# Output projection by column halves, expert weights loaded into the homes that come free, and a router that chooses in one pass

## The chip, the cores and the metric

The kernel runs on one core of a Trainium2 chip. The metric is device microseconds (us) of one execution; the median of several executions is compared. One core has a matrix engine (TensorE, in the rows PE, its weight loads PEld), a vector engine (VectorE, DVE), an activation engine (ScalarE, ACT), GpSimd (POOL) and a queue engine (SyncE, SP) that issues most transfers. All of them run their own instruction streams and wait for each other through semaphores.

## The reference

Two transformer blocks run one after the other on 512 tokens of width 1024, in float32. What matters here is the end of the second block: the output projection of its mixer, and a mixture of 32 experts in 4 groups of 8.

```python
h = h + z @ w_o                                   # mixer's output projection, 1024 x 1024
u = rmsnorm(h, norm_ffn_g)
g_logits = u @ w_group + b_group                  # 4 groups
p_grp, g_sel = top_k(softmax(g_logits), 1)
e_logits = (u @ w_router + b_router).reshape(n, 4, 8)
in_grp = e_logits of the chosen group             # 8 experts
p_exp, e_sel = top_k(softmax(in_grp), 2)
gate = p_grp * p_exp / sum(p_exp)
out[token] += gate * ((silu(x @ w1[e]) * (x @ w3[e])) @ w2[e])   # for both chosen experts
return rmsnorm(h, norm_final_g)
```

Each expert's w1, w3 and w2 are 2 MB each (1024 x 512 or 512 x 1024 in float32).

## The kernel before

Nearly all of SBUF is one array `M` of 128 partitions by 53200 words; every tile is a fixed stretch of it, a "home" (`at(offset, shape)`), so whether a transfer can start is a question of who last used its home. 1 MB is 2048 words of every partition. PSUM is `PS`, 8 banks of 512 words.

**Output projection (`out_pe`, `out_act`, `out_dve`).** The 512 tokens are NT = 4 tiles of 128. For each tile and each half of the 1024 output columns there is one job (`HN_JOBS`, the tile outermost): `rows` makes 8 products with `WO` (each appears as two matrix rows in the trace, L2964) and adds the residual `hT` by 4 small products with the identity (L2967). ACT copies the bank into `HN` (L3010), and after the second half of a tile makes the root mean square of the row (square, Ln, table load, Exp: L3016 to L3020); DVE scales the row into `UN` (L3044), and ACT stores it to `u_rows` in HBM (`store`, L3006). Between the jobs PE turns a finished tile (`turn`, 8 transposes, L2976), DVE copies the turned tile to `UT` (L3035), and PE makes its 36 router and group logits (`logits`, L2983). The last two tiles' turns and logits stand behind the last job. Then all four engines meet at a barrier (`stage`, L257).

**Routing (`route_dve`, `route_pe`).** DVE finds for all tiles the best group, then the best and second-best expert in it (`first_best`, L3216 to L3220, three times; one instruction each, followed by a wait for its result), and gives the chosen experts as ones in `ES` (L3237, `routing_given`). PE counts them by matrix products (L3185, L3187), DVE works out each token's slot, PE names the rows of each pair of experts (L3193), DVE writes the list (L3291, L3292), and POOL gathers the first pair's rows from `u_rows` (L3404). While PE waits it runs `keep_busy`: products with the identity whose result nobody reads (L356; 6 calls are 12 matrix rows).

**Experts (`experts_sp`, `experts_pe`).** Expert k and expert k + 16 form a pair; each takes 64 rows, so a pair fills the array's 128 columns. There are 16 pairs here. `w1_w3` makes the w1 product and signals `h_one`, then the w3 product and signals `h_done`; `w2` turns the hidden rows, multiplies by w2 and signals `y_done`. All three are L3443 in the trace. w1 has two homes (`W1B[0]`, `W1B[1]`), w3 and w2 have one each. So SP issues the next pair but one's w1 at `h_one`, the next pair's w3 at `h_done`, and its w2 at `y_done`: 12 MB a pair. Pair 0's w1 and w3 are issued at the start of the output projection. Pair 1's w3 goes to three 1 MB homes named `SPARE` and, for its last megabyte, to W3B after pair 0's `h_done`:

```python
sp.wait_ge(stage_done, WORKERS * (PROJ2_STAGE + 4))   # behind the output projection
gate_weights(1, (1, BASE + 1), of=(0,))               # 2 MB
sp.wait_ge(u_stored, U_STORED)
down_weights((0, BASE))                               # 4 MB
sp.wait_ge(g_in, 16)                                  # the first rows are gathered
...                                                   # GFIN 0.5 MB, w1 2 MB, two spares 2 MB
sp.wait_ge(stage_done, WORKERS * (PROJ2_STAGE + 5))
spare_part(2, 1, 1)                                   # 1 MB
```

**End.** SP loads the experts' rows back (`CG`, 4 x 1 MB, L3617), DVE adds them weighted (L3578), normalises with `GFIN` (L3572), and SP stores the output.

Of the kernel before, what the change touches and what calls it, by code (L numbers as in the profile page):

```python
# [23 lines left out]
P = 128  # L24
# [100 lines left out]
def gain_columns(inputs):  # L125
# [9 lines left out]
    bias = np.concatenate([np.asarray(inputs["b_group_2"])[0], np.asarray(inputs["b_router_2"])[0]])  # L135
# [60 lines left out]
def program(nc, I, out, dbg=None, stop=99):  # L196

    ctx = ExitStack()
    with ctx:
# [1600 lines left out]
        WO = at(WORK0 + 5280, KD, D)  # L1800
# [1155 lines left out]
        HN_JOBS = [(t, half) for t in range(NT) for half in range(2)]  # L2956
# [3 lines left out]
        def out_pe(pe):  # L2960
            def rows(n, t, half):
                lo = OUT_TILES[t][0]
                for a in range(KD):
                    nc.tensor.matmul(PS[:, n % 2, :], ZT[:, a, lo:lo + P], WO[:, a, 512 * half:512 * half + 512],  # L2964
                                     start=a == 0, stop=False)
                for a in range(4):
                    last = nc.tensor.matmul(PS[:, n % 2, a * P:a * P + P], hT[:, 4 * half + a, lo:lo + P], ident,  # L2967
                                            start=False, stop=a == 3)
                last.then_inc(hn_ready, 1)

            def turn(t):
                pe.wait_ge(hn_free, 2 + 2 * t + 2)
                if t >= 2:
                    pe.wait_ge(ut_out, t - 1)
# [3 lines left out]
                last.then_inc(ut_ready, 1)  # L2978

            def logits(t):  # L2980
                pe.wait_ge(ut_out, t + 1)
                for a in range(KD):
                    last = nc.tensor.matmul(PS[:, 6, 36 * t:36 * t + 36], UT[:, a, P * t:P * t + P], RW[:, a, :],  # L2983
                                            start=a == 0, stop=a == KD - 1)
                last.then_inc(lg_ready, 1)

            pe.wait_ge(wo_in, 16)
            for n, (t, half) in enumerate(HN_JOBS):
                pe.wait_ge(hn_free, n + 1)
                rows(n, t, half)  # L2990
                if half == 0 and t >= 2:
                    logits(t - 2)
                if half == 1 and t >= 1:
                    turn(t - 1)
            turn(NT - 1)
            logits(NT - 2)
            logits(NT - 1)

        def out_act(act):
# [8 lines left out]
            for n, (t, half) in enumerate(HN_JOBS):  # L3008
                act.wait_ge(hn_ready, n + 1)
                nc.scalar.activation(HN[:, t, 512 * half:512 * half + 512], PS[:, n % 2, :], ACT.Copy).then_inc(hn_free, 1)  # L3010
                if half == 0:
                    if t > 0:
                        store(t - 1)
                    continue
                act.drain()
# [9 lines left out]
        def out_dve(dve):  # L3025
# [6 lines left out]
            def turned(t):  # L3032
                dve.wait_ge(ut_ready, t + 1)
                for c in range(2):
                    nc.vector.tensor_copy(UT[:, 4 * c:4 * c + 4, P * t:P * t + P],  # L3035
                                          PS[:, 2 + 2 * (t % 2) + c, :].rearrange("p (a n) -> p a n", n=P))
                dve.drain().then_inc(ut_out, 1)

            for t in range(NT):
                if t == NT - 1:  # L3040
                    turned(NT - 2)
                    turned(NT - 1)
# [3 lines left out]
                if 0 < t < NT - 1:  # L3046
                    turned(t - 1)


        def mix2_sp(sp):  # L3050
# [3 lines left out]
            sp.dma_start(WO, I["w_o_2"].rearrange("(a p) n -> p a n", p=P)).then_inc(wo_in, 16)  # L3054
# [23 lines left out]
        def mix2_dve(dve):  # L3078
# [7 lines left out]
            out_dve(dve); stage(dve, "dve")  # L3086
# [5 lines left out]
        XG, YO = at(HT0, D), at(HT0 + 1024, D)  # L3092
        UT = at(XN0, KD, S1)
        W1B = [[at(WORK0 + 18592 + 4096 * k, KD, DE) for k in range(2)], [at(XN0, KD, DE), at(WORK0 + 8192, KD, DE)]]
        W3B = [at(WORK0 + 26784 + 4096 * k, KD, DE) for k in range(2)]
        W2B = [at(WORK0 + 4096 * k, 4, D) for k in range(2)]
        SPARE = [at(WORK0 + 12288, 4, DE), at(HT0 + 2048, 4, DE), at(RG0 + 2560, 4, DE)]
        UN = [at(RG0, D), at(RG0 + 1024, D), at(WORK0, D), at(WORK0 + 13472, D)]
        JUNK = at(HT0, D)
# [12 lines left out]
        LG = small(NT, 36)  # L3112
        OHG, GE = small(NT, 4), small(NT, 4)
        EL, EL2, OH1, OH2 = small(NT, 8), small(NT, 8), small(NT, 8), small(NT, 8)
# [4 lines left out]
        C5 = {n: small(NT) for n in ("gmax", "gsum", "mx", "m1", "m2", "ex", "den", "ga1", "ga2", "ss", "rs")}  # L3119
        C10 = {n: small(2 * NT) for n in ("rank", "pair", "half", "ob", "q", "in", "eid", "step", "last")}  # L3120
# [5 lines left out]
        CG = [at(base + 2 * D * n, 2, D) for base in (XN0, WORK0 + 8192) for n in range(2)]  # L3126
        GFIN = GROW
        LAST_SLOTS = [at(HT0 + 2048 + P * n, P) for n in range(2 * NT)]
        LAST_GATES = at(HT0 + 3072, S1)
# [31 lines left out]
        def route_sp(sp):  # L3161
            sp.wait_ge(stage_done, WORKERS * (PROJ2_STAGE + 3))
            sp.dma_start(GROW, I["norm_ffn_g_2"].to_broadcast([P, D])).then_inc(rw_in, 16)
            sp.dma_start(RW[:, :, 0:4], wcols("w_group_2", 0, 4)).then_inc(rw_in, 16)
            sp.dma_start(RW[:, :, 4:36], wcols("w_router_2", 0, 32)).then_inc(rw_in, 16)
# [14 lines left out]
        def route_pe(pe):  # L3180
            keep_busy(6, 7)
# [17 lines left out]

        def route_dve(dve):  # L3200
# [6 lines left out]
            dve.wait_ge(lg_ready, NT)  # L3207
            for t in range(NT):
                stt(LG[:, t, :], PS[:, 6, 36 * t:36 * t + 36], C5["rs"][:, t:t + 1], g["router_bias"], ALU.mult, ALU.add)
            nc.vector.memset(ES[:, NT, :], 0.0)  # L3210
            dve.drain()
            G, EG = LG[:, :, 0:4], LG[:, :, 4:36].rearrange("p t (g e) -> p t g e", g=4)

            def first_best(values, best, order, n, dest, place):

                then(nc.vector.reduce_max(best, values, axis=AX))  # L3216
                then(tt(dest, values, bc(best, n), ALU.is_equal))
                then(tt(dest, dest, over(order, NT), ALU.mult))
                then(nc.vector.reduce_max(place, dest, axis=AX))
                then(tt(dest, dest, bc(place, n), ALU.is_equal))  # L3220


            first_best(G, C5["gmax"], C["g4"], 4, OHG, C5["mx"])

            T4 = T48.rearrange("p t (g e) -> p t g e", g=4)
            then(tt(T4, EG, OHG.unsqueeze(3).to_broadcast([P, NT, 4, 8]), ALU.mult))
            then(nc.vector.reduce_sum(EL, T48.rearrange("p t (g e) -> p t e g", g=4), axis=AX))
            first_best(EL, C5["m1"], C["g8"], 8, OH1, C10["eid"][:, 0:NT])
            then(stt(EL2, OH1, -BIG, EL, ALU.mult, ALU.add))
            first_best(EL2, C5["m2"], C["g8"], 8, OH2, C10["eid"][:, NT:2 * NT])  # L3230

            for j, oh in enumerate((OH1, OH2)):
                tt(E12[:, j].rearrange("p t (g e) -> p t g e", g=4), OHG.unsqueeze(3).to_broadcast([P, NT, 4, 8]),
                   oh.unsqueeze(2).to_broadcast([P, NT, 4, 8]), ALU.mult)
            ts_(STEP64, C["iota"][:, 1:9], float(ROWS), None, ALU.mult)
            dve.drain()
            tt(ES[:, 0:NT, :], E12[:, 0], E12[:, 1], ALU.add).then_inc(routing_given, 1)  # L3237
# [5 lines left out]
            counted = float(8 * 4 + 8)  # L3243
            for j in range(2):
                chosen = C10["eid"][:, NT * j:NT * j + NT]
                stt(chosen, C5["mx"], -8.0, chosen, ALU.mult, ALU.subtract)
            dve.drain()
# [4 lines left out]
            tt(GE, G, bc(C5["gmax"], 4), ALU.subtract).then_inc(choice_in, 1)  # L3252
            tt(C5["ex"], C5["m2"], C5["m1"], ALU.subtract).then_inc(choice_in, 1)
# [29 lines left out]

            dve.wait_ge(choice_out, 1)
# [41 lines left out]
        def experts_sp(sp):  # L3326
# [35 lines left out]
            up_weights((0, BASE))  # L3362
            sp.wait_ge(stage_done, WORKERS * (PROJ2_STAGE + 4))
# [388 lines left out]
```

## Time and profile before

| | |
|---|---|
| median of 3 executions | 2332.2 us (2331.75 to 2332.29) |
| the profiled execution | 2332.89 us |
| its span, first to last instruction | 2331.1 us |
| mean granted TensorE clock | 0.982 |
| PE busy | 2172.8 us (93%) |
| output projection | 1736 to 1811.7 us of the span |
| routing, until the first rows are there | 1811.7 to 1833.3 us |
| experts | 1834 to 2308 us |

Times in the rows are us from the first instruction of the profiled execution. A busy PE is not PE at its peak, because matrix rows are pipelined; how long an engine stood idle before an instruction, and what released it, says more than its share of busy time.

### The profile page before, as it was taken

The numbers are of one execution on the slowest core, as the hardware profiler recorded it, in microseconds if no ns is written. First come the engines' busy times: TensorE is split into PE (matmuls) and PEld (weight loads), VectorE is DVE, ScalarE is ACT, GpSimd is POOL, SyncE is SP. The second block draws the span as 40 slices with busy tenths as digits, with TensorE's granted clock in tenths as the row PEclk, the third lists the DMA queues.
The fourth block names the chain that finished last, engine by engine and source line by source line (L and its number), as shares of the span: only waits on it lengthen the run. The fifth ranks groups of instructions, "written<-read, shape, count | busy, mean of one in ns | idle before, by whom it ended". The sixth has DMA issues, their size and how long they took to land.

```text
span 2331.1 us, 25184 instructions
## 1 busy us (share of the span) xinstructions
PE 2172.8 (93%) x9688; PEld 1451.1 (62%) x9688; DVE 990.1 (42%) x1993; ACT 434.4 (19%) x818; POOL 108.1 (5%) x139
## 2 busy tenths in 40 slices
PE   8999999999989999999999999899999988777786
PEld 6888888545657788888764666556875433222232
DVE  6555444124777554543443246867641400000014
ACT  2010000145362110100021113552112000000001
POOL 0000000000101000000020000210000000000000
PEclk9999999999999999999999999999999998998999
DMA  5132232311021322322124122001242899999997
GB/s 160 55 99 83 73 100 82 105 36 36 1 91 65 99 91 73 106 98 86 64 63 106 36 73 68 5 12 55 82 164 119 330 423 427 427 427 427 426 381 311
DMA packets 173722, 347.50 MB, mean 149 GB/s; under 512 B 18099, under 2 KB 144179, under 8 KB 153138
## 3 DMA queue, kind: packets, MB, share of 16 engines
q1 hardware_dynamic: 167536, 331.66, 38.3%
q0 software_dynamic: 5504, 12.32, 1.5%
q10 hardware_dynamic: 578, 2.10, 0.2%
q8 instruction: 69, 1.13, 0.2%
q14 instruction: 35, 0.29, 0.0%
HBM read 337.33 MB, written 16.26 MB: 152 GB/s over the span
## 4 chain that ended last, share of the span: by engine, by line
PE 70%; DMA 17%; DVE 6%; issue 3%; ACT 2%; DVEq 1%; SPq 1%; ACTq 0%; POOL 0%; POOLq 0%
PE PS L636 19%; DMA M<-w 11%; PE PS L667 10%; PE PS L3443 7%; PE PS L73 6%; PE PS L2791 5%; DMA M<-w_ffn_up 4%; PE PS L2964 2%; PE PS L1000 2%; PE PS L415 2%; PE PS L1576 1%; PE PS L1948 1%; PE PS L1027 1%; PE PS L970 1%; PE PS L337 1%
## 5 line engine op out<-in xcount | busy, mean ns | idle before, releaser
L636 PE MATMUL PS<-M 128*128 128x256 f32 x2464 | 537.1, 380 | 3.3 <-DMA M<-w_ffn_up 1.4
L636 PEld LDWEIGHTS PS<-M 128*128 128x128 f32 x2464 | 466.6, 190 | 74.5 <-DMA M<-w_ffn_up 8.9
L3443 PE MATMUL PS<-M 128*64 128x512 f32 x1536 | 361.9, 630 | 84.0 <-DMA M<-w 60.9
L3443 PEld LDWEIGHTS PS<-M 128*64 128x64 f32 x1536 | 114.1, 145 | 319.3 <-issue 216.6
L667 PE MATMUL PS<-M 128*128 128x256 f32 x1232 | 268.7, 379 | 5.5 <-DVE M L825 3.1
L667 PEld LDWEIGHTS PS<-M 128*128 128x128 f32 x1232 | 233.4, 190 | 42.6 <-issue 11.3
L3543 DVE TENSOR_TENSOR M<-M,PS 128x512 f32<-128x512 f32 x16 | 11.0, 687 | 410.2 <-PE PS L3443 410.2
L762 DVE TENSOR_TENSOR M<-M,PS 128x256 f32<-128x256 f32 x220 | 92.6, 421 | 200.1 <-PE PS L636 195.7
L73 PE MATMUL PS<-M 128*128 128x264 f32 (+1 forms) x486 | 158.3, 484 | 0.6 <-ACT M L314 0.6
L2791 PE MATMUL PS<-M 128*128 128x256 f32 x616 | 134.9, 380 | 3.8 <-DVE M L2891 1.8
L2791 PEld LDWEIGHTS PS<-M 128*128 128x128 f32 x616 | 115.8, 190 | 22.5 <-DVE M L2891 2.3
L73 PEld LDWEIGHTS PS<-M 128*128 128x128 f32 x486 | 91.1, 190 | 61.8 <-issue 50.0
L712 DVE TENSOR_TENSOR M<-M 128x512 f32<-128x512 f32 (+1 forms) x68 | 48.0, 705 | 119.3 <-DMA M<-w_ffn_down 100.8
L697 ACT ACTIVATE M<-M 128x256 f32<-128x256 f32 x66 | 27.5, 417 | 325.1 <-DVE M L762 325.1
L3522 ACT ACTIVATE M<-PS 128x1024 f32<-128x1024 f32 x16 | 16.4, 1024 | 349.0 <-PE PS L3443 349.0
L321 POOL TENSOR_TENSOR M<-M 128x512 f32<-128x512 f32 (+1 forms) x20 | 27.7, 1387 | 934.1 <-ACT M L314 910.8
L2964 PE MATMUL PS<-M 128*128 128x512 f32 x128 | 58.2, 609 | 2.1 <-DVEq L257 2.1
L1000 PE MATMUL PS<-M 128*128 128x512 f32 x128 | 56.1, 595 | 0.0
L1576 PE MATMUL PS<-M 128*128 128x256 f32 x224 | 50.7, 383 | 3.4 <-DVE M L1625 1.8
L713 DVE TENSOR_TENSOR M<-M 128x512 f32<-128x512 f32 (+1 forms) x68 | 49.7, 731 | 0.0
L1576 PEld LDWEIGHTS PS<-M 128*128 128x128 f32 x224 | 41.8, 190 | 12.4 <-issue 4.6
L715 DVE TENSOR_TENSOR M<-M 128x512 f32<-128x512 f32 (+1 forms) x68 | 46.0, 676 | 6.3
(401 smaller groups left out, 2267.8 us busy)
## 6 DMA issues: line engine op xcount, KB each, us to landing
M<-w SPq DMA_DIRECT2D x128, 1024.0 KB, 19.1
M<-w SPq DMA_DIRECT2D x32, 2048.0 KB, 24.3
M<-w_ffn_gate SPq DMA_DIRECT2D x22, 1024.0 KB, 5.4
M<-w_ffn_up SPq DMA_DIRECT2D x22, 1024.0 KB, 5.3
M<-w_ffn_down SPq DMA_DIRECT2D x16, 1024.0 KB, 5.1
M<-w_in SPq DMA_DIRECT2D x27, 512.0 KB, 3.8
M<-w_in SPq DMA_DIRECT2D x12, 1024.0 KB, 5.3
M<-w_ffn_down SPq DMA_DIRECT2D x8, 768.0 KB, 4.4
```

Of the source, the lines that this page charges most:

```text
L73: last = nc.tensor.matmul(PS[lo:lo + m, bank + c, 0:self.n], lhsT, rhs[:, c * self.n:(c + 1) * self.n], start=start, stop=stop)
L415: last = nc.tensor.matmul(PS[:, 4 + n % 2, :], slot(s, 0, KD, P)[:, a, :], xnT[:, a, 0:S1], start=a == 0, stop=a == KD - 1)
L636: last = nc.tensor.matmul(PS[:, 3 * half + BANK[p], 0:HALF], lhs[:, a, :], rhs[:, a, :], start=p in FIRST and a == 0, stop=p in LAST and a ...
L667: last = nc.tensor.matmul(down_bank(name), lhs[:, c, :], rhs[lo + c], start=q == 0 and c == 0, stop=q == len(DOWN_PARTS) - 1 and c == n - 1)
L712: nc.vector.tensor_tensor(wsum(m, "S1"), A(1, 0), A(1, 1), ALU.add).then_inc(weights_summed, 1)
L713: nc.vector.tensor_tensor(wsum(m, "S3"), A(0, 0), A(1, 0), ALU.subtract).then_inc(weights_summed, 1)
L762: nc.vector.tensor_tensor(dest, a, b, ALU.add).then_inc(block_taken, 1)
L1000: last = nc.tensor.matmul(PS[:, bank, :], slot(s, k * KD * P, KD, P)[:, a, :], xnT[:, a, 0:S1], start=a == 0, stop=a == KD - 1)
L1576: last = nc.tensor.matmul(out_bank(j, name), lhs[:, a, :], rhs[:, a, :], start=a == 0, stop=a == 3)
L2791: last = nc.tensor.matmul(gbank(c, BANK[p]), lhs[:, a, :], rhs[:, a, :], start=p in ("P1", "P6", "P5") and a == 0, stop=p in ("P2", "P4", ...
L2964: nc.tensor.matmul(PS[:, n % 2, :], ZT[:, a, lo:lo + P], WO[:, a, 512 * half:512 * half + 512], start=a == 0, stop=False)
L3443: last = nc.tensor.matmul(PS[ROWS * k:ROWS * k + ROWS, bank, :], wide[:, a * P + ROWS * k:a * P + ROWS * k + ROWS], weights(k), start=star ...
```

## The change

The output projection's jobs run by column halves: the first half of all four tiles, then the second half. `WO` becomes two tiles of 512 columns each, loaded by two transfers. When the first half is copied out (`hn_free` at 2 + NT), the home of its weights (`WORK0 + 9376`) and the first half of `hT` (`HT0`) are free, and SP issues there pair 1's second w1 (2 MB) and one spare megabyte of w3. `turn` and `logits` of the tile before now stand inside the second-half jobs of tiles 1 to 3 (ahead of products 2 and 6), and PSUM signals go by half tiles. The router's choice (`choose_dve`) runs on 40 columns at once, 4 groups of 8 experts and the 4 groups themselves padded to 8: best and second best in every group of eight, multiplied by the chosen group afterwards. It is called for tiles 0 and 1 inside the output projection and for tiles 2 and 3 behind the barrier. The arithmetic of the gates' exponents moves behind the slots' arithmetic. The last megabyte of pair 1's w3 gets homes of its own (`SPARE_ROWS`, `SPARE_ROW`), and the load of `GFIN` moves to the end.

```diff
-        HN_JOBS = [(t, half) for t in range(NT) for half in range(2)]
+        HN_JOBS = [(t, half) for half in range(2) for t in range(NT)]
...
                 for a in range(KD):
-                    nc.tensor.matmul(PS[:, n % 2, :], ZT[:, a, lo:lo + P], WO[:, a, 512 * half:512 * half + 512],
+                    if half == 1 and t > 0 and a == 2:
+                        turn(t - 1)
+                    if half == 1 and t > 0 and a == KD - 2:
+                        logits(t - 1)
+                    nc.tensor.matmul(PS[:, n % 2, :], ZT[:, a, lo:lo + P], WO[half][:, a, :],
                                      start=a == 0, stop=False)
...
             for n, (t, half) in enumerate(HN_JOBS):
                 pe.wait_ge(hn_free, n + 1)
                 rows(n, t, half)
-                if half == 0 and t >= 2:
-                    logits(t - 2)
-                if half == 1 and t >= 1:
-                    turn(t - 1)
             turn(NT - 1)
-            logits(NT - 2)
             logits(NT - 1)
...
+            for t in range(NT - 1):
+                turned(t)
+                normed(t)
+            choose(0, NT - 2)
+            turned(NT - 1)
+            normed(NT - 1)
...
         def route_pe(pe):
-            keep_busy(6, 7)
+            keep_busy(6, 5)
             pe.wait_ge(routing_given, 1)
...
+            for j, logits in enumerate((LG, LG2)):
+                values, dest = by_eight(logits[:, tiles, :]), by_eight(CHOICE[:, j, tiles, :])
+                best, place = flat(BEST[:, j, tiles, :]), flat(PLACE[:, j, tiles, :])
+                then(nc.vector.reduce_max(best, values, axis=AX))
+                then(tt(dest, values, bc(best, 8), ALU.is_equal))
+                then(tt(dest, dest, order, ALU.mult))
+                then(nc.vector.reduce_max(place, dest, axis=AX))
+                then(tt(dest, dest, bc(place, 8), ALU.is_equal))
+                if j == 0:
+                    then(stt(by_eight(LG2[:, tiles, :]), dest, -BIG, values, ALU.mult, ALU.add))
...
+            choose_dve(dve, NT - 2, 2)
...
-            tt(GE, G, bc(C5["gmax"], 4), ALU.subtract).then_inc(choice_in, 1)
-            tt(C5["ex"], C5["m2"], C5["m1"], ALU.subtract).then_inc(choice_in, 1)
...
+            tt(GE, LG[:, :, 32:36], bc(BEST[:, 0, :, 4], 4), ALU.subtract).then_inc(choice_in, 1)
+            then(tt(BY_GROUP, BEST[:, :, :, 0:4], by_choice_group, ALU.mult))
+            then(nc.vector.reduce_sum(by_choice(C10["top"]), BY_GROUP, axis=AX))
+            then(tt(C5["ex"], C10["top"][:, NT:2 * NT], C10["top"][:, 0:NT], ALU.subtract)).then_inc(choice_in, 1)
             dve.wait_ge(choice_out, 1)
...
+            sp.wait_ge(hn_free, 2 + NT)
+            gate_weights(1, (1, BASE + 1), of=(1,))
+            spare_part(1, BASE + 1, 0)
             sp.wait_ge(stage_done, WORKERS * (PROJ2_STAGE + 4))
             gate_weights(1, (1, BASE + 1), of=(0,))
             sp.wait_ge(u_stored, U_STORED)
             down_weights((0, BASE))
             sp.wait_ge(g_in, 16)
-            sp.dma_start(GFIN, I["norm_final_g_2"].rearrange("(o n) -> o n", o=1).to_broadcast([P, D])).then_inc(gains_in, 16)
-            gate_weights(1, (1, BASE + 1), of=(1,))
-            spare_part(0, 1, 0)
-            spare_part(1, BASE + 1, 0)
+            for piece in range(2):
+                sp.dma_start(SPARE[0][piece], expert("w3_2", 1, KD)[:, 2 * piece:2 * piece + 2, :]).then_inc(spare_in, 16)
             sp.wait_ge(stage_done, WORKERS * (PROJ2_STAGE + 5))
             spare_part(2, 1, 1)
+            sp.dma_start(SPARE_ROWS, expert("w3_2", BASE + 1, KD)[:, 4:7, :]).then_inc(spare_in, 16)
+            sp.dma_start(SPARE_ROW, expert("w3_2", BASE + 1, KD)[:, 7:8, :]).then_inc(spare_in, 16)
             sp.wait_ge(h_one, 1)
             gate_weights(0, (2, BASE + 2))
             sp.wait_ge(h_done, 1)
-            sp.sem_inc(w3_in[0], 32)
-            sp.sem_inc(w3_in[1], 16)
-            up_part(W3B[1][:, KD // 2:KD, :], BASE + 1, 1)
+            for part in range(2):
+                sp.sem_inc(w3_in[part], 32)
```

## Rows read from the trace of the kernel before

**Rows 1.** The page: mean busy share of the DMA engines, tenths, 40 slices.
```profile
DMA  5132232311021322322124122001242899999997
```

**Rows 2.** Stretches: us, busy of PE, PEld, DVE, ACT, POOL, clock, DMA share, GB/s.
```profile
1780.00:1800.00 20.00, 20.00 (x78) 11.34 (x77) 2.48 (x3) 5.41 (x8) 0.00 (x0) 1.00 0.07 27
...
1840.00:1860.00 20.00, 18.60 (x92) 7.72 (x90) 2.51 (x3) 0.60 (x1) 1.19 (x2) 1.00 1.00 424
```

**Rows 3.** Issues of transfers by SP in order of time (start, us).
```profile
1833.27 0.33 SPq L3368 DMA_DIRECT2D M<-norm_final_g  x1
...
1861.67 2.14 SPq L3343 DMA_DIRECT2D M<-w  x4
...
1875.40 1.75 SPq L3329 DMA_DIRECT2D M<-w  x4
```

**Rows 4.** Chain that ended last, in order of time (start, us, what).
```profile
1769.17 0.87 PE PS L2976 x8
...
1777.80 1.71 PE PS L2983 x16
...
1835.89 15.65 PE PS L3443 x64
...
1854.54 20.84 PE PS L3443 x96
...
1876.72 20.67 DMA M<-w
```

**Rows 5.** Stretches of 2 us (busy of POOL, clock, DMA share, GB/s).
```profile
1860.00:1862.00 2.00, 0.00 (x0) 1.00 0.99 410
1862.00:1864.00 2.00, 0.18 (x2) 1.00 0.86 254
```

**Rows 6.** PE in order of time, end of the projection and routing.
```profile
1807.81 3.76 PE L2983 MATMUL PS<-M 128*128 128x36 f32 x32 [0.50 <-DVEq L3037]
1811.68 7.11 PE L356 MATMUL PS<-M 128*128 128x512 f32 x12
...
1819.25 0.97 PE L3187 MATMUL PS<-M 128*128 128x128 f32 x8
1820.06 5.40 PE L356 MATMUL PS<-M 128*128 128x512 f32 x12
```

**Rows 7.** ACT in order of time: last copy out, and the last store's issue.
```profile
1805.56 0.60 ACT L3010 ACTIVATE M<-PS 128x512 f32<-128x512 f32 x1 [8.95 <-PE PS L2967]
...
1810.66 0.33 ACTq L3006 DMA_DIRECT2D u_rows<-M  x1
```

**Rows 8.** DVE in order of time, last scaled row and routing.
```profile
1809.34 1.28 DVE L3044 SCALAR_TENSOR_TENSOR M<-M 128x1024 f32<-128x1024 f32 x1 [0.21 <-ACT M L3020]
...
1815.22 0.19 DVE L3217 TENSOR_TENSOR M<-M 128x32 f32<-128x32 f32 x1
1815.49 0.19 DVE L3218 TENSOR_TENSOR M<-M 128x32 f32<-128x32 f32 x1
...
1818.52 0.29 DVE L3237 TENSOR_TENSOR M<-M 128x128 f32<-128x128 f32 x1
...
1820.33 0.42 DVE L3260 TENSOR_TENSOR M<-M,PS 128x256 f32<-128x256 f32 x1
...
1828.02 0.19 DVE L3291 TENSOR_SCALAR M<-PS 128x31 f32<-128x31 f32 x1 [0.53 <-PE PS L3193]
```

**Rows 9.** Stretches of 1 us, PE alone (busy, clock, DMA share, GB/s).
```profile
1813.00:1814.00 1.00, 1.00 (x3) 0.50 0.43 131
...
1833.00:1834.00 1.00, 0.70 (x6) 1.00 0.00 0
...
1837.00:1838.00 1.00, 1.00 (x4) 0.50 1.22 496
```

**Rows 10.** The end: stretch of 2 us (as rows 5).
```profile
2310.00:2312.00 2.00, 0.00 (x0) 1.00 0.43 172
```

**Rows 11.** The end in order of time: the first final normalisation.
```profile
2317.41 1.28 DVE L3572 SCALAR_TENSOR_TENSOR M<-M 128x1024 f32<-128x1024 f32 x1
```

More of the change, by code:

```diff
@@ L3011, in out_act @@
                 if half == 0:
-                    if t > 0:
-                        store(t - 1)
                     continue
+                if t > 0:
+                    store(t - 1)
                 act.drain()
@@ L3023, in out_act, with out_dve @@
             store(NT - 1)
-        def out_dve(dve):
+        def out_dve(dve, choose):
             nc.vector.memset(CMP[:, 0:D], 0.0)
@@ L3053, in mix2_sp @@
             sp.wait_ge(e_av, NT)
-            sp.dma_start(WO, I["w_o_2"].rearrange("(a p) n -> p a n", p=P)).then_inc(wo_in, 16)
+            for half in range(2):
+                sp.dma_start(WO[half], wcols("w_o_2", 512 * half, 512)).then_inc(wo_in, 16)
         def mix2_pool(pool):
@@ L3118, in program @@
         BE = [small(32), small(32)]
-        C5 = {n: small(NT) for n in ("gmax", "gsum", "mx", "m1", "m2", "ex", "den", "ga1", "ga2", "ss", "rs")}
-        C10 = {n: small(2 * NT) for n in ("rank", "pair", "half", "ob", "q", "in", "eid", "step", "last")}
+        C5 = {n: small(NT) for n in ("gsum", "ex", "den", "ga1", "ga2", "ss", "rs")}
+        C10 = {n: small(2 * NT) for n in ("rank", "pair", "half", "ob", "q", "in", "eid", "step", "last", "top")}
         LAST_PAIR = small(1)
@@ L3125, in program @@
         IDX, IDY = small(1, dt=I32), small(1, dt=I32)
[L3126 to L3129, printed above, removed]
+        CG = [at(base + 2 * D * n, 2, D) for base in (XN0, WORK0 + 9376) for n in range(2)]
+        GFIN = at(WORK0 + 8192, D)
+        LAST_SLOTS = [at(HT0 + P * n, P) for n in range(2 * NT)]
+        LAST_GATES = at(HT0 + 1024, S1)
         u_dram = nc.dram_tensor("u_rows", (S1 + 1, D), F32, kind="Internal").ap()
@@ L3206, in route_dve @@
             tt, ts_, stt = nc.vector.tensor_tensor, nc.vector.tensor_scalar, nc.vector.scalar_tensor_tensor
-            dve.wait_ge(lg_ready, NT)
-            for t in range(NT):
-                stt(LG[:, t, :], PS[:, 6, 36 * t:36 * t + 36], C5["rs"][:, t:t + 1], g["router_bias"], ALU.mult, ALU.add)
             nc.vector.memset(ES[:, NT, :], 0.0)
[L3211 to L3234, printed above, removed]
             ts_(STEP64, C["iota"][:, 1:9], float(ROWS), None, ALU.mult)
-            dve.drain()
-            tt(ES[:, 0:NT, :], E12[:, 0], E12[:, 1], ALU.add).then_inc(routing_given, 1)
+            choose_dve(dve, NT - 2, 2)
+            group = CHOICE[:, 0, :, 32:36]
+            by_choice_group = group.unsqueeze(1).to_broadcast([P, 2, NT, 4])
             def by_choice(column):
```

95 lines of the change are left out of this document (61 added, 34 removed).

## The prediction, made before the changed kernel ran

> **What bounds the kernel now.** I read the page's slices first: the DMA engines are at 0 to 5 tenths in the first 31 of the 40 slices, at 2 in the slice that holds the output projection (1748 to 1807), at 8 in the next and at 9 in all but the last of the rest [rows 1]. This last fifth is the experts, and there bytes are the limit: 424 GB/s, share 1.00 [rows 2]. Before it lies a stretch in which almost nothing is moved, 27 GB/s [rows 2], while PE does the output projection. That picture invites the sum "bytes that move from the full stretch into the empty one, divided by 424 GB/s". Whether it holds is a question of where the full stretch starts to be what the end waits for, and the chain of waits answers that, not the share of busy time.
>
> The chain [rows 4] runs through PE without a break from the first product of pair 0 (1835.89) over w2 of pair 0 and w1 and w3 of pair 1 (1854.54, 20.84 us), and only at 1876.72 does it step to a transfer: pair 2's w3, which SP issues at 1875.40 [rows 3], at pair 1's `h_done`. So from 1835.9 to 1875.4 PE waits for no weights at all. And what is queued ahead of that w3? SP issues pair 1's w2 at 1861.67, when pair 0's `y_done` frees its home, and pair 3's w1 after it. If the queue is still full of older requests at 1861.67, these stand in line and fewer old bytes help; if it has just run dry, they don't. The stretches of 2 us show it run dry: 410 GB/s until 1862, then 254 [rows 5]. I can check it by bytes: from 1833.27 SP issues 0.5 MB (GFIN), 2 MB of w1, three spare megabytes, 4 MB for pair 2's w1 and the last megabyte of w3, 10.5 MB or 11.0 million bytes; at 424 GB/s that is 26.0 us. Nothing moves before 1834 [rows 9], and two gathers of at most half a megabyte each lie between (up to 2.5 us), so it ends between 1860 and 1862.5. Backlog at 1861.67: about 1 us, no more than the delay that the new request has anyway. In front of 1861.67 the transfers are busy, but nobody waits for them.
>
> So the end is set, backwards, by: a full queue from 1862 on; its start at pair 0's `y_done`; PE's unbroken work since the first gathered rows; the routing; the barrier at 1811.68; the output projection. What shifts pair 0's `y_done` shifts the end by as much, and nothing else in this change can.
>
> **The change part by part.**
>
> *Three megabytes into freed homes, the fourth spare megabyte, GFIN away.* The requests between 1833 and 1862 shrink by 3.5 MB, from 10.5 to 7. At 424 GB/s this is 8.7 us of queue. By the reading above they only make the queue run dry earlier, and pair 1's w2 still starts when its home comes free. Value: a gain of 0.2 us, because the new request then meets an idle queue; ends 0 and 0.9 us (the backlog in [rows 5]). The early 3 MB fall into the empty stretch [rows 2] and are there long before use. What is issued behind the gathered rows and the second barrier is 3 MB, there by about 1843 (7.4 us of queue), and first needed at pair 1's products, behind 1861.7. SP's new wait (`hn_free`, about 1770) has behind it only requests that wait for the barrier at 1811.7 anyway. GFIN moves behind the four loads of expert rows; the transfers end at about 2312.8 (172 GB/s in 2310 to 2312, [rows 10]), half a megabyte more is 1.3 us, so it lands near 2314, and its first reader starts at 2317.41 [rows 11]. Value 0; without that cover it would cost 1.3 us.
>
> *Order of the jobs.* In the old order a turn and the logits of a tile stand ahead of the last job only for tiles 0 and 1; tile 2's and 3's come behind it. In the new one tile 2's turn and logits are inside the last job or ahead of it too. On the chain one turn is 0.87 us and one tile's logits 1.71 [rows 4], and the job behind logits starts 0.08 us slower (6.95 against 6.87 in the chain): the last copy out moves from 1805.56 [rows 7] by 2.66 to 1808.22. What follows is ACT's and DVE's chain for the last tile, which the change does not shorten: copy, square, Ln, table load, Exp, then DVE's scaling at 1809.34 [rows 8], then the issue of the store at 1810.66, 5.10 us behind the copy's start, 0.33 long [rows 7]. New: issue at 1813.32, done 1813.65. Before, PE's logits of two tiles ended at 1811.57 and the barrier opened at 1811.68 [rows 6]; they hid ACT's chain. New, PE has one turn and one tile's logits behind the last copy: copy 0.6, turn 1.0, a copy of 0.7, logits of which half overlaps, some 3.6 us, so 1812, well ahead of ACT. The barrier is now ACT's: 1813.65 plus 0.1 to 0.3, I take 1813.85. Cost: 2.17 us (ends 1.9 and 2.7). The turns and logits inside the jobs wait for work that is 1 to 3 us old by then, so I cost those waits at 0; if PE had to wait for each, they would cost some tenths three times. `choose` for tiles 0 and 1 runs on DVE from about 1803 for 5 us, while DVE has nothing else until about 1809.4.
>
> *Choice behind the barrier.* Before, DVE needs from 1811.68 to 1818.81 [rows 6, 8], 7.13 us. New: two clears and one small product, two scalings (0.8 us together), then 11 steps that each wait for the one before. A step on 32 elements starts 0.27 us after its predecessor, and from 32 to 256 elements the duration grows from 0.19 to 0.42 [rows 8], 1.03 ns an element; on 80 elements it is 0.32. That is 3.5 us, and two products and a sum at the end 0.7: 5.0 us. DVE gains 2.1 us. But PE also has to get there: it runs the same twelve rows of `keep_busy`, 7.11 us, from 1811.68 to 1818.79 [rows 6], and its next product stood ready within 0.1 us of DVE's signal. With the same twelve rows and the same clock PE now is the later one and the gain is 0.1 us. At the full clock they take 5.40 us (the second set, [rows 6]), and the gain would be 1.7, the end opposite. The difference is the granted clock: 0.50 at 1813 [rows 9], which is the 1.2 GHz level, after 3.8 us in which PE had only the 36-column logits. In the new order PE idles or runs small products for 5.6 us ahead of the barrier (1808.2 to 1813.85), so I expect the half clock again. The DVE arithmetic behind the choice has two waited steps more (+0.25 us), hidden under PE's product, which ends 8.5 us behind the barrier (before: 1820.22, [rows 6]) while DVE is ready after 6.8.
>
> The Trainium skill, "TensorE: Matmul & The Clock Gate", section on the clock gate, says the low clock is the default state and activity releases it. The trace agrees: 0.50 at 1813 follows the logits. By the rule the low clock comes back at both places for certain; then the half microsecond that I allow for the clock below falls away, and the sum would end at 2334.5.
>
> *Gates' exponents.* Four steps now stand between the last slot product and the list (GE, a product, a sum, a difference; 0.08 and three times 0.27, 0.9 us), and the wait for ACT's answer adds about 0.1. DVE idled 0.53 us at this place [rows 8]. Cost 0.48 us (ends 0.3 and 0.7).
>
> *Clock later.* Before, a second half-clock stretch lies in pair 0's first product (0.50 at 1837, [rows 9]). It costs 1.75: 64 rows took 15.65 us, while 96 later ones took 20.84, or 13.9 for 64 [rows 4]. Both stretches follow idling of the same kind as before, but where they fall against the work shifts by 2 us. Together I take 0.5 us of gain; ends 3.4 of gain (neither costs: 1.7 and 1.75) and 1.7 of loss (one more).
>
> **Sum.** +2.17 - 0.1 + 0.48 - 0.2 + 0 - 0.5 = +1.85 us. The profiled execution took 2332.89, 0.7 above the median; it would take 2334.7. On the median of 2332.2: 2334.0 us.
>
> **Rivals.**
>
> *A, bytes count (faster).* If the full queue did hold back the chain from 1834 on, 3.5 MB less are worth 8.7 us: 2332.2 - 8.7 + 2.05 = 2325.6, 0.3% faster. For it: the share of 1.00 from 1840 [rows 2]. Against it: the dip at 1862 and the chain through PE [rows 4, 5]. It would need a backlog of 6 us at 1861.67. Chance 0.1.
>
> *B, PE runs its rows in the routing at half clock throughout (slower).* Twelve rows wholly at half clock are twice 5.40, 10.8 us, 3.7 more than now, with pair 0's product as before: 2.17 - 0.1 + 0.48 - 0.2 + 3.7 = 6.05 us, 2338.2. It passes 4.7 us when the half clock costs the routing 4.1 us instead of 1.7, so when it lasts 8 us behind the barrier. For it: less work on PE ahead of the barrier. Against it: the twelve rows themselves ended it before. Chance 0.1.
>
> *C, the routing does get shorter.* Full clock behind the barrier and in pair 0: 2.17 - 1.7 + 0.48 - 0.2 - 1.75 = -1.0, 2331.2. No change by measurement; part of my forecast's range, a quarter of its 0.8.
>
> **How the numbers follow.** About 0.2% (4.7 us) is what a measurement of this kernel can tell from no change. Forecast with C 0.8, A 0.1, B 0.1. Range: from C less a microsecond for the unknown backlog, 2330, to B's 2337.5; it leaves out A and part of B. Faster by over 0.2%: 0.11; slower: 0.10; within: 0.79.
>
> **What would show it.** Right: SP issues 3 MB near 1770; the last copy out at 1808, the barrier near 1813.9 and opened by ACT; PE, not DVE, late at the first count; the queue idle for 4 to 6 us before pair 1's w2; pair 0's `y_done` 1 to 3 us later than 1861.67, and the end shifted by the same. Wrong: `y_done` unmoved and the end earlier (A), or the twelve rows over 8 us (B). Later pairs that change their spacing of 31 us would mean a mechanism that I have not seen.

## The result and the profile after

The changed kernel takes 2336.64 us in the median of 20 executions (2332.42 to 2340.7), the kernel before 2332.4 of 20; the ratio is 1.0015, 95% interval 1.0009 to 1.0021, so 3.5 us more (2.1 to 4.9); the two medians themselves are 4.2 us apart. 2334.0 was forecast, with a range of 2330 to 2337.5. The execution that was profiled took 2338.07 us, 5.2 more than the one of before, and its span is 5.1 us longer. The page after, span and mean DMA share by slice:

```profile
span 2336.2 us, 25205 instructions
...
DMA  4132222311021322322124122001244699999997
```

The slice of the output projection went from 2 to 4 tenths and the next fell from 8 to 6 [rows 1]: bytes did move forward. SP's issues of the changed kernel (start, us):

```profile
1773.52 0.33 SPq L3371 DMA_DIRECT2D M<-w  x1
1773.89 0.43 SPq L3356 DMA_DIRECT2D M<-w  x1
1817.56 0.33 SPq L3371 DMA_DIRECT2D M<-w  x1
...
1838.22 0.80 SPq L3395 DMA_DIRECT2D M<-w  x2
...
1850.80 0.80 SPq L3371 DMA_DIRECT2D M<-w  x2
1867.76 2.03 SPq L3366 DMA_DIRECT2D M<-w  x4
...
1881.49 1.75 SPq L3352 DMA_DIRECT2D M<-w  x4
```

The 3 MB go out at 1773.5. Behind pair 2's w1 (1850.80) nothing can be issued until pair 0's `y_done` frees w2's home at 1867.76, and the queue runs dry ahead of it. Stretches of 2 us after (busy of POOL, clock, DMA share, GB/s):

```profile
1860.00:1862.00 2.00, 1.01 (x1) 1.00 0.97 418
1862.00:1864.00 2.00, 0.00 (x0) 1.00 0.55 176
1864.00:1866.00 2.00, 0.00 (x0) 1.00 0.01 2
1866.00:1868.00 2.00, 0.00 (x0) 1.00 0.00 0
```

In the kernel before the queue ran dry within a microsecond behind its `y_done` [rows 5]; now it runs dry some 4 us ahead of it and stands empty for about 5 us. That is where the early megabytes went. PE, ACT and DVE at the end of the projection and in the routing, after:

```profile
1811.92 0.60 ACT L3011 ACTIVATE M<-PS 128x512 f32<-128x512 f32 x1 [5.38 <-PE PS L2971]
...
1817.01 0.33 ACTq L3007 DMA_DIRECT2D u_rows<-M  x1
```

```profile
1814.01 1.98 PE L2989 MATMUL PS<-M 128*128 128x36 f32 x16 [0.35 <-DVE M L3036]
1817.58 5.42 PE L356 MATMUL PS<-M 128*128 128x512 f32 x12 [1.60 <-ACTq L257]
...
1823.11 0.97 PE L3192 MATMUL PS<-M 128*128 128x128 f32 x8
...
1838.25 1.16 PE L3181 MATMUL PS<-M 128*128 128x128 f32 x8 [2.04 <-DMA M<-u_rows,M]
```

```profile
1822.04 0.23 DVE L3243 TENSOR_TENSOR M<-M 128x64 f32<-128x64 f32 x1
...
1832.28 0.19 DVE L3314 TENSOR_SCALAR M<-PS 128x31 f32<-128x31 f32 x1
```

The projection starts at 1739.86 here, 3.69 us later than before. Less this, the last copy out is at 1808.23, the store's issue at 1813.32 and the barrier at 1813.89; 1808.22, 1813.32 and 1813.85 were forecast. PE's own last row ends at 1815.99, and it then idles 1.60 us for ACT. DVE has its choice ready at 1822.27, 4.7 us behind the barrier (5.0 forecast, 7.1 before), and PE comes 0.6 us after it, at the end of its twelve rows, though these ran at full clock this time. The chain of waits goes on from there:

```profile
1830.41 0.29 DVE M L3301
...
1833.99 4.22 DMA M<-u_rows,M
...
1840.84 16.79 PE PS L3468 x64
...
1860.63 20.84 PE PS L3468 x96
...
1882.81 20.25 DMA M<-w
```

The gather takes 4.22 us (3.5 before), and pair 0's 64 rows 16.79, against 15.65 [rows 4]. As before, PE works on without a transfer from pair 0's first product until it needs pair 2's w3, issued at 1881.49.

### The profile page after: what moved, and what is told of

It reads as the page before. It is cut to its first block, busy times and chain, and to the rows that moved or that the text cites. A ratio compares the mean times of both kernels' runs of the same rounds, so it can differ in the third digit from the quotient of the medians.

```text
span 2336.2 us, 25205 instructions
## 1 busy us (share of the span) xinstructions
PE 2176.5 (93%) x9688; PEld 1453.0 (62%) x9688; DVE 993.2 (43%) x2005; ACT 434.7 (19%) x818; POOL 108.7 (5%) x139
## 4 chain that ended last, share of the span: by engine, by line
PE 71%; DMA 15%; DVE 5%; issue 3%; ACT 2%; DVEq 1%; SPq 1%; PEld 1%; ACTq 0%; PEldq 0%; POOL 0%; POOLq 0%
PE PS L636 22%; DMA M<-w 11%; PE PS L667 10%; PE PS L3468 7%; PE PS L73 6%; PE PS L2791 5%; PE PS L2968 2%; PE PS L1000 2%; PE PS L415 2%; PE PS L1948 1%; DMA M<-w_ffn_up 1%; PE PS L1027 1%; PE PS L970 1%; PE PS L337 1%; DMA M<-expert_rows 1%
```

## One table for all runs

Two executions of one kernel lie up to 8.3 us apart, which is more than most terms of the sum. So each profile is cut at four events: PE's first row of the projection ("start"), the first unread row behind the barrier ("barrier"), pair 0's `y_done`, and the end of the span. Times in us; the ratio is that of the whole times to those of the kernel before on the same chip, with its 95% interval.

| run | start | start to barrier | barrier to y_done | y_done to end | ratio |
|---|---|---|---|---|---|
| before | 1736.2 | 75.5 | 50.0 | 469.4 | |
| e4 (before) | 1738.4 | 75.5 | 49.9 | 469.1 | 0.9999 (0.9990 to 1.0008) |
| e11 (before) | 1734.6 | 73.8 | 49.9 | 469.6 | |
| after | 1739.9 | 77.7 | 50.2 | 468.4 | 1.0015 (1.0009 to 1.0021) |
| e0 (after) | 1739.3 | 76.0 | 50.5 | 468.6 | 1.0013 (1.0004 to 1.0022) |
| e1 late loads | 1741.9 | 77.7 | 51.9 | 468.6 | 1.0012 (1.0003 to 1.0021) |
| e2 old order | 1744.4 | 75.1 | 47.6 | 468.3 | 0.9997 (0.9988 to 1.0006) |
| e3 old tail | 1737.0 | 76.3 | 48.7 | 468.4 | 1.0009 (1.0000 to 1.0018) |
| e5 more rows | 1740.5 | 76.0 | 49.3 | 468.4 | 0.9998 (0.9989 to 1.0007) |
| e6 late, +2 MB | 1741.1 | 76.0 | 50.5 | 472.7 | 1.0026 (1.0015 to 1.0036) |
| e7 after, +2 MB | 1741.7 | 77.7 | 50.4 | 468.7 | 1.0010 (1.0001 to 1.0019) |
| e8 w3 early | 1737.9 | 76.0 | 52.5 | 463.3 | 0.9987 (0.9978 to 0.9996) |
| e9 late, w3 early | 1738.2 | 77.7 | 51.8 | 466.3 | 1.0001 (0.9992 to 1.0010) |
| e10 combined | 1734.4 | 75.1 | 48.1 | 462.1 | 0.9965 (0.9952 to 0.9979) |

"Start to barrier" has two values 1.7 us apart for one and the same code (75.5 and 73.8; 77.7 and 76.0): a stretch of half clock (1.2 GHz) lies in the first job, whose products with `WO` then take 8.83 us, or doesn't, and they take 7.13.

## The experiments

**e0: the changed kernel again; e4 and e11: the kernel before again.**

> The changed kernel once more, for a second profile. The part up to the output projection is the same code as before; in the first pair of profiles it was 3.7 us longer in the changed kernel (1739.8 against 1736.1). If that is chance, it comes out anywhere within some us of 1736 here; if the change causes it, it comes out near 1740 again. From the start of the output projection to the end: 596.4 us in the first profile of the changed kernel, 595.0 before; I expect 596 to 597.

> The kernel before once more, for a second profile. Its first profile reached the output projection at 1736.2 us; the five profiles with the new code stand at 1737.0 to 1744.4, apart by stretches of half clock at 650, 717, 1160, 1460 and 1500 us, in code that no change touches. If these are chance, this profile falls between 1736 and 1744; if the new code brings them, it stands at 1736 again. From the projection's start to the end: 594.9 us in the first; within 2 us of that here. Pair 0's y_done to the end: 469.4.

> The kernel before a third time, for a third profile of its part up to the output projection (1736.2 and 1738.4 us so far; eight profiles with the new code: 1737.0 to 1744.4, mean 1740.7). Chance: anywhere between 1736 and 1744. If the old code keeps this part short, it stands at 1736 to 1739.

The part from the start to the end repeats within 1.6 us for the old kernel (593.3 to 594.9) and within 1.1 for the changed one (595.2 and 596.3; e0 was expected at 596 to 597). In the old kernel the difference is the half clock in the first job; in the changed one that stretch, the twelve rows behind the barrier and pair 0's first product trade places. The part ahead of the start is code that the change leaves alone, and it varies from 1734.6 to 1738.4 with the old kernel and from 1734.4 to 1744.4 over eleven profiles with the new code. Stretches of half clock near 717, 1457 and 1495 us stand in e4 too, so the old code isn't free of them, and e3 and e10 with the new code have none ahead of the start. e11 was expected between 1736 and 1744 either way and came below that. Most of the 5.1 us between the first two profiles (3.7) is this part. Whether its mean is the same in both (1736.4 of three, 1739.7 of eleven) stays open; three profiles are too few.

**e1: the 3 MB issued late.**

```diff
-            sp.wait_ge(hn_free, 2 + NT)
-            gate_weights(1, (1, BASE + 1), of=(1,))
-            spare_part(1, BASE + 1, 0)
...
             sp.wait_ge(g_in, 16)
+            gate_weights(1, (1, BASE + 1), of=(1,))
+            spare_part(1, BASE + 1, 0)
```

> The changed kernel, but the 3 MB that it loads into the homes of the first half are issued behind the first gathered rows. Theory (nobody waits for transfers before pair 0's y_done): 6 MB are then issued behind the rows, 14.8 us of queue with pair 2's w1 behind them, done before y_done at +29 us; time within 0.5 us of the changed kernel, and pair 0's y_done as far behind the barrier as there. Rival A (bytes count): 3 MB more in the full stretch, 7.4 us slower than the changed kernel.

Ratio 1.0012 against e0's 1.0013, and 468.6 us behind `y_done` in both. The early issue of 3 MB is worth nothing in this kernel, against 7.4 us by rival A. The queue of e1, stretches of 2 us with `y_done` at 1871.47:

```profile
1868.00:1870.00 2.00, 0.00 (x0) 1.00 1.04 442
1870.00:1872.00 2.00, 0.00 (x0) 1.00 0.39 154
1872.00:1874.00 2.00, 0.34 (x2) 1.00 0.74 176
```

It runs dry some 0.7 us ahead of `y_done`, where the kernel before did so just behind it. Its routing was 1.4 us longer than e0's in this one profile: 1.0 is the clock (twelve rows of 8.13 us instead of 7.11), the rest mostly a slower gather (4.48 against 4.25 to PE's first transposition).

**e6 and e7: 2 MB more that nobody reads, on both.**

```diff
+        waste = nc.dram_tensor("waste", (P, KD, DE), F32, kind="Internal").ap()
...
             sp.wait_ge(g_in, 16)
+            sp.dma_start(waste, expert("w1_2", 5, KD)).then_inc(waste_in, 16)
```

> e1_late_loads with a copy of 2 MB from HBM to HBM that nobody waits for, issued behind the first gathered rows. In e1 the queue ran dry less than a microsecond before pair 0's y_done. Theory: now it is still busy at y_done, 4 us or more (2.1 million bytes at 424 GB/s are 4.9 us, and a copy within HBM may cost up to twice that), so pair 1's w2 and all behind it land that much later: y_done as in e1, the rest behind y_done and the whole time 4 to 9 us longer. This is the point from which bytes count.

> The changed kernel with the same copy of 2 MB. Its queue stood empty for about 5 us before pair 0's y_done. Theory: the copy fills that gap; time and the stretch behind y_done (468.4 to 468.6 us) as in the changed kernel, within 1 us, or up to 4 us longer should a copy within HBM take twice its bytes. Rival A: 4.9 us slower, like e6.

e6, whose queue had no room left, takes 4.1 us more behind `y_done` (472.7 against 468.6); e7, whose queue stood empty, takes 468.7. In e6 the queue is full across `y_done` (1867.62), in e7 it still has a gap ahead of it (1869.75):

```profile
1866.00:1868.00 2.00, 0.00 (x0) 1.00 1.04 440
1868.00:1870.00 2.00, 0.18 (x1) 1.00 1.05 443
```

```profile
1866.00:1868.00 2.00, 0.00 (x0) 1.00 0.50 201
1868.00:1870.00 2.00, 0.00 (x0) 1.00 0.02 6
```

The first two lines are e6, the last two e7. The whole times agree: 1.0026 for e6 against 1.0010 for e7, two intervals that overlap by 0.04%. So bytes count from the point at which the queue is still busy at `y_done`, and the kernel before stood just at that point.

**e2: the old order of the jobs with all of the new routing, the 3 MB late.**

```diff
-        HN_JOBS = [(t, half) for half in range(2) for t in range(NT)]
+        HN_JOBS = [(t, half) for t in range(NT) for half in range(2)]
...
                 rows(n, t, half)
+                if half == 0 and t >= 2:
+                    logits(t - 2)
+                if half == 1 and t >= 1:
+                    turn(t - 1)
             turn(NT - 1)
+            logits(NT - 2)
             logits(NT - 1)
```

> The jobs in the old order (tile outermost, the last two tiles' turns and logits behind the last job), with the new choice of experts, the fourth spare megabyte and the later GFIN kept and the 3 MB loaded late. Theory: from the start of the projection the barrier opens 75.5 us later as before the change (77.8 in the changed kernel), the choice behind it is 1.6 us shorter than before, the end 1 to 2 us earlier than before the change and 2.2 us earlier than with the new order. If the order of the jobs costs nothing, it equals the changed kernel.

The cut shows PE's part; ACT's stores, DVE's copies and the wait ahead of a turn go back to the old order with it, and the loads are those of e1. The barrier is back at 75.06 us behind the start, 2.66 us ahead of the new order with the same clock (77.72). From the start to the end it takes 590.9 us, 3.7 to 4.0 less than the 594.6 and 594.9 of the old kernel with the same half-clock stretch, more than the 1 to 2 expected, because neither the twelve rows nor pair 0's first product met the half clock. Against e1, which differs from it in the order alone and ran on the same chip, its median is 2.7 us lower (2334.28 against 2336.97 us, 11 executions each; the intervals of their two ratios overlap by 0.03%). Against the kernel before the median shows no gain (0.9997), and its interval reaches 0.12% below; the profile was one with a late start (1744.4). So the cost of the order is shown by the cut and borne out by the whole times; a gain of the rest over the kernel before is neither shown nor excluded by them.

**e3: the new order, but tile 2's turn and logits behind the last job.**

```diff
-                    if half == 1 and t > 0 and a == 2:
+                    if half == 1 and 0 < t < NT - 1 and a == 2:
                         turn(t - 1)
...
                 rows(n, t, half)
+            turn(NT - 2)
             turn(NT - 1)
+            logits(NT - 2)
             logits(NT - 1)
...
-            for t in range(NT - 1):
+            for t in range(NT - 2):
                 turned(t)
                 normed(t)
+            normed(NT - 2)
             choose(0, NT - 2)
+            turned(NT - 2)
             turned(NT - 1)
             normed(NT - 1)
```

> The changed kernel, but tile 2's turn and logits stand behind the last job again, so that they cover ACT's chain for the last tile. Theory: the last copy out 2.66 us earlier (69.4 us behind the start of the projection instead of 72.1), the barrier 2.1 us earlier (75.6 instead of 77.8) and opened by PE and ACT within 0.5 us of each other, the end 2.2 us earlier than the changed kernel. If the barrier were set by PE's work alone, nothing would change.

The last copy out comes 69.4 us behind the start, 2.65 earlier, as expected. The barrier comes at 76.3, 1.4 us earlier and not 2.1. PE and DVE show why:

```profile
1806.21 1.95 PE L2980 MATMUL PS<-M 128*128 128x128 f32 x16
1809.18 3.98 PE L2989 MATMUL PS<-M 128*128 128x36 f32 x32 [1.03 <-DVE M L3038]
```

```profile
1808.30 0.23 DVE L3247 TENSOR_TENSOR M<-M 128x64 f32<-128x64 f32 x1
1808.45 2.48 DVE L3038 COPY M<-PS 128x512 f32<-128x512 f32 x4
```

DVE was still at the choice for tiles 0 and 1 when PE had turned tile 2, and PE waited 1.03 us for the copy, which in the kernel before cost it 0.50 [rows 6]. From the start to the end it takes 593.4 us, 2.9 less than the changed kernel, more than the 2.2 expected, because the half clock missed pair 0's first product here. The ratio of 1.0009 lies below e0's 1.0013, but well inside its interval: the whole time shows no gain. e10 puts the choice ahead of tile 2's scaling; its barrier is at 75.1.

**e5: 14 instead of 10 unread rows ahead of the gathered rows.**

```diff
-            keep_busy(5, 7)
+            keep_busy(7, 7)
             transpose_rows(pe, 16)
```

> The changed kernel with 14 instead of 10 rows of unread products between the naming of the rows and the gathered rows (7 calls for 5). PE idled 2.0 us there. Theory of the clock: with about 0.3 us of idling, pair 0's first product takes 7.1 us instead of 8.6 to 10.0, so y_done falls 1.5 to 2.8 us earlier behind the barrier, and the end with it. If the half clock comes from elsewhere (PE's wait behind the barrier and DVE's copy, 1.5 us), the product takes 8.6 to 10.0 again.

```profile
1832.36 6.25 PE L356 MATMUL PS<-M 128*128 128x512 f32 x14
1839.21 1.16 PE L3181 MATMUL PS<-M 128*128 128x128 f32 x8 [0.60 <-DMA M<-u_rows,M]
1841.81 13.95 PE L3468 MATMUL PS<-M 128*64 128x512 f32 x64 [1.43 <-DVE M L3567]
```

PE idles 0.60 us instead of 2.04, and the 64 rows of pair 0 take 13.95 us, against 16.79 in the changed kernel's chain. From their start to `h_one` it is 7.1 us against 8.5 to 10.1 in the seven profiles with the changed kernel's projection and routing (after, e0, e1, e6 to e9). The granted clock is 1.00, the 2.4 GHz level, without a break, and 1.4 to 2.9 us are saved by two calls of work that nobody reads. e2, e3 and e10 say the same: PE idled 0.57, 0.35 and 0.25 us there, and pair 0's first product took 7.1 us. In e2 and e3 the half clock fell into the ten unread rows themselves, which made them 1.7 us longer and so took the idling away (e2's):

```profile
1833.52 6.24 PE L356 MATMUL PS<-M 128*128 128x512 f32 x10
```

The ratio of 0.9998 against e0's 1.0013 agrees, though the two intervals overlap.

**e8 and e9: pair 2's w3 issued at pair 0's `h_done`.** Its home has been free there since the fourth spare megabyte; the changed kernel lets it lie idle until pair 1's `h_done`.

```diff
             for part in range(2):
                 sp.sem_inc(w3_in[part], 32)
+            up_weights((2, BASE + 2))
             sp.wait_ge(y_done, 1)
             down_weights((1, BASE + 1))
-            pair(2, 1)
+            sp.wait_ge(h_one, 2)
+            gate_weights(1, (3, BASE + 3))
+            sp.wait_ge(y_done, 2)
+            down_weights((2, BASE + 2))
```

> The changed kernel, with pair 2's w3 issued at pair 0's h_done instead of pair 1's. Its home is free there only because all of pair 1's w3 now lies in spare homes. Theory: it fills the 5 us in which the queue stood empty before pair 0's y_done, and the queue then stays full to the end: y_done as in the changed kernel, from y_done to the end 463 to 464 us instead of 468.6, time 5 us shorter than the changed kernel, 0.1% below the kernel before. If the queue's idle time is not what the end waits for, nothing changes.

> e1_late_loads (3 MB behind the gathered rows) with the same early issue of pair 2's w3. Its queue was empty for less than 1 us before y_done. Theory: y_done to the end 467.5 to 468.5 us instead of 468.6, so 4 us more than e8_up2_early: only now do the 3 MB in the freed homes gain their time. If e8's gain came from the order of the transfers and not from the gap, e9 gains as much.

e8: the queue is full across `y_done` (1866.40),

```profile
1862.00:1864.00 2.00, 0.00 (x0) 1.00 0.98 414
1864.00:1866.00 2.00, 0.00 (x0) 1.00 1.04 432
1866.00:1868.00 2.00, 0.18 (x1) 1.00 0.98 414
```

the rest takes 463.3 us, 5.3 less than in e0, and the kernel is 0.13% faster than before (0.04 to 0.22), although its routing was 2.0 us longer than e0's (pair 0's first product took 10.05 us instead of 8.55, the gather 0.5 more). With the 3 MB late (e9) the same edit gives 2.3 us, 466.3; the forecast was at most 1.1. The two low stretches of e1 account for it: 154 and 176 GB/s for 4 us are 2.4 us less than a full queue moves. The queue fills slowly once it has been empty: in the 3 us behind e1's `y_done` it moves 62, 123 and 360 GB/s. Between e8 and e9 lie 3.0 us: now, and only now, the homes of the first half gain time.

**e10: what the runs point to.** e3's tail with the choice ahead of tile 2's scaling, 5 calls of unread products ahead of the first count, 7 ahead of the gathered rows, and e8's issue.

```diff
+            turn(NT - 2)
             turn(NT - 1)
+            logits(NT - 2)
             logits(NT - 1)
...
-            for t in range(NT - 1):
+            for t in range(NT - 2):
                 turned(t)
                 normed(t)
             choose(0, NT - 2)
+            normed(NT - 2)
+            turned(NT - 2)
             turned(NT - 1)
             normed(NT - 1)
...
-            keep_busy(6, 5)
+            keep_busy(5, 5)
...
-            keep_busy(5, 7)
+            keep_busy(7, 7)
...
+            up_weights((2, BASE + 2))
```

> The changed kernel with what the runs point to: tile 2's turn and logits behind the last job, DVE's choice for tiles 0 and 1 ahead of tile 2's scaling, 5 instead of 6 calls of unread products ahead of the first count and 7 instead of 5 ahead of the gathered rows, and pair 2's w3 issued at pair 0's h_done. Theory: barrier 75.4 us behind the projection's start, y_done 47 to 49 us behind the barrier, together 122.4 to 124.4 instead of 125.5 before the change, and y_done to the end 463 to 464 instead of 469.3: 7 to 9 us faster than the kernel before, 0.3 to 0.4%.

```profile
1805.36 3.66 PE L2989 MATMUL PS<-M 128*128 128x36 f32 x32
1809.44 6.25 PE L356 MATMUL PS<-M 128*128 128x512 f32 x10 [0.43 <-ACTq L257]
...
1824.37 6.25 PE L356 MATMUL PS<-M 128*128 128x512 f32 x14
1830.87 1.16 PE L3185 MATMUL PS<-M 128*128 128x128 f32 x8 [0.25 <-DMA M<-u_rows,M]
1833.47 13.95 PE L3476 MATMUL PS<-M 128*64 128x512 f32 x64 [1.43 <-DVE M L3575]
```

Median 2322.32 us of 5 executions against 2332.33 of 21, ratio 0.9965 (0.9952 to 0.9979): 8.2 us faster than the kernel before (4.9 to 11.2) by the ratio. From the start to the end it takes 585.3 us; the kernel before takes 593.3 with its best clock (e11) and 594.9 in its first profile, 8.0 and 9.6 more. 7 to 9 were expected. Barrier and `y_done` came as expected, and behind `y_done` it was 0.9 us better than the range of 463 to 464; no run says why. How the gain divides between its edits was not tried one by one.

## Why the prediction was right, and where its sum was off

The forecast was that the bytes would not count and that the order of the jobs would cost about 2 us, and both hold. By its own steps, with the means of the three profiles of the old kernel and of the seven that have the changed kernel's projection and routing (after, e0, e1, e6, e7, e8, e9):

- *Early megabytes.* Forecast: a gain of 0.2 us, ends 0 and 0.9. Measured behind `y_done`: 469.4 to 468.6, so 0.8, the upper end. e1 and e2, which issue the 3 MB late, have it too (468.6 and 468.3), so it isn't their early issue. Pair 2's w3 lands 35.6 us behind `y_done` in the mean of the three old profiles and 35.5 in that of after, e0, e1, e2, e3, e5 and e7 (35.72 and 35.30 in the first profile of each kernel), so at the point that the forecast spoke of the gain is about 0.2, as forecast. The other 0.6 comes later, in the full stretch, and no run shows from what. Rival A's 8.7 us are refuted by e1, e6 and e7.
- *GFIN at the end.* Forecast 0. From the landing of the expert rows to the end it is 24.1 us before and 24.0 to 24.1 after, so 0.
- *Order of the jobs.* Forecast +2.17, measured +2.2 (77.7 against 75.5). The steps were right one by one: PE's 2.66 us ahead of the last copy, and ACT's chain, no longer covered, as what opens the barrier. By e2 the order alone costs 2.66, and the rest of the new projection code, presumably its signals by half tiles, gives 0.45 back (75.06 against 75.51); the forecast took the order for 2.17 and the rest for nothing.
- *Choice behind the barrier.* Forecast: DVE 2.1 us shorter, the path 0.1. DVE was 2.4 us shorter. The path from the barrier to PE's first count took 7.2 us in each old profile and 6.8 in the mean of the seven (5.3 to 8.0), so the gain was 0.4. It is a matter of the clock: the twelve rows took 5.42, 7.11, 8.13, 7.11, 5.42, 7.11 and 8.18 us, against 7.11 before.
- *Gates' exponents.* Forecast +0.48. From the start of the last slot product to the list it is now 1.87 us (1830.41 to 1832.28) and was 1.46 (1826.56 to 1828.02), so +0.41; from the first count to the gather's issue, which holds this term and the steps ahead of it, +0.3.
- *What the sum lacked.* The gather took longer: issue to PE's first transposition 3.5 to 3.6 us in the three profiles of the old kernel, 4.2 to 4.7 in all eleven with the new code. In the mean of the seven that is +0.9, and it makes PE idle longer ahead of pair 0.
- *Clock later.* Forecast a gain of 0.5 for the two half-clock stretches of the routing together, beside the 0.1 above. Measured: 0.3 gained in the twelve rows beyond that 0.1, and 0.4 lost in pair 0's first product, which took 8.8 us before and 9.2 in the mean of the seven (three of them near 10, four at 8.5 to 8.8). So the two come to about nothing, and the gain of half a microsecond was not there. PE idled 2.0 to 2.5 us ahead of that product in the seven and 0.9 before; e5 shows that without the idling it runs at full clock. The Trainium skill, "TensorE: Matmul & The Clock Gate", section on the clock gate, says that the low clock is the default state and activity releases it. The trace agrees in pair 0, where all seven met the half clock; behind the barrier two of the seven did not, so the prediction's "for certain" does not hold there.

Together: +2.2 up to the barrier, from barrier to `y_done` 49.9 to 51.1 so +1.2 (-0.4, +0.3, +0.9 and +0.4), and -0.8, which is +2.6 us. The forecast of +1.85 came close by the path that it named, but partly by luck: the gather (+0.9) and the missing gain of the clock (+0.6 with the choice) were made good in part by the 0.6 behind `y_done` that was not foreseen. The comparison of whole times says 3.5 (2.1 to 4.9); what is left, if it is not chance, would lie ahead of the projection.

Rival B did not come: the twelve rows never took 10.8 us. Its sign, over 8 us, did appear in two of the seven (e1 and e9, 8.13 and 8.18), which is 1.0 us of the 3.7 that B asks for. B's own sum gives 2338.2, so the range up to 2337.5 stopped short of it. C came in half: full clock behind the barrier in two of seven, never in pair 0.

## What to carry to other kernels

A queue that is busy is not yet a queue that somebody waits for. Before counting bytes that move forward, find the first transfer on the chain and ask what was in line ahead of it when it was issued; here a home that came free late (w2) reset the queue, and 3 MB moved ahead of that point were worth nothing until another request was moved across it as well. Work that stands behind the last job may be there to cover another engine's chain; pulled forward it adds its time to the chain (2.7 us here) and saves nothing behind the last job.

## What the runs showed of the hardware that I had not expected

**A gather is slower with a packet of instructions among its own.** The gather of pair 0's rows takes 3.4 to 3.5 us to landing in the three profiles of the old kernel and 4.1 to 4.7 in all eleven with the new code. DMA queues in 3.3 us around it, after, and then in 2.8 us around it before (queue, kind, packets, MB, share; then issue, KB, us to landing):

```profile
q0 software_dynamic: 144, 0.25, 28.6%
q1 hardware_dynamic: 9, 0.03, 2.4%
q14 instruction: 1, 0.01, 0.6%
...
M<-u_rows,M POOLq DMA_INDIRECT x1, 4.2
```

```profile
q0 software_dynamic: 144, 0.25, 34.7%
...
M<-u_rows,M POOLq DMA_INDIRECT x1, 3.5
```

The same 144 packets, and one packet of instructions of 8 KB among them. The nine packets of q1 are the last of pair 0's w2. They are not the cause: in e1 and e9 w2 had landed 0.6 us ahead of the gather's issue, and the gather still took 4.44 and 4.22 us. The packet of instructions starts 2.3 to 2.9 us behind the gather's issue in all eleven profiles with the new code, and 6.8 to 6.9 us behind it, after the landing, in the three with the old. That the packet is the cause is argued from this coincidence alone and was not tried by moving the code, and no run shows why the fetch comes 4 us earlier with the new code.

**The same code varies by up to 10 us ahead of the change.** Near 650, 717, 1157, 1457 and 1495 us a stretch of half clock appears in some executions and not in others. One such stretch in the first job is worth 1.7 us. They are not all of it: three profiles without any of them ahead of the projection (e10, the first of the old kernel, e3) start it at 1734.4, 1736.2 and 1737.0 us. It took 11 to 20 executions of each kernel to see 3 us in whole times; cut at four events, one profile shows it to some tenths.
